# A hybrid decoder step: the delta-rule front moved beside the input projection, and the cache keys re-staged

## The reference, cut to what matters

```python
qa, ka, va, qb, kb, vb, fb, qc, kc, vc, zc, ac, bc, ud, vd = project(h, w_in)      # 1024 -> 3084 columns
o_a = combine_by_denominator([dilated(q, k, v, w, d) for (w, d) in ((128,1),(512,4),(2048,16))])  # A: sliding windows (SWA)
o_b = fox_attend(qb, kb_all, vb_all, cum_t, ...)                 # B: forgetting attention (FoX), all past keys
o_c, s_c, conv_c = gdn_branch(qc, kc, vc, ac, bc, ...)           # C: short conv, l2 norm, chunked delta rule
o_d, v_d = gmlp_branch(ud, vd, ws, bs, gv)                       # D: spatial gating
y = concat([norm(o_a), norm(o_b), norm(o_c) * silu(z_c), norm(o_d)]) @ w_out
```

```python
a_mat = where(strict, (k*beta) @ k.T * decay, 0);  t_mat = inverse(eye + a_mat)
u = t_mat @ (v * beta);  w = t_mat @ (k*beta*exp(gcum));  qk = (q @ k.T) * decay
v_new = u - w @ s;  o = (q*exp(g)) @ s + qk @ v_new;  s = s*exp(g_last) + (k*exp(g_last-g)).T @ v_new
```

## Time and profile before

| | |
|---|---|
| median of the runs (3) | 1573.7 us (1571.72 to 1576.14) |
| the profiled execution | 1572.86 us |
| its span, first to last instruction | 1571.0 us |
| mean granted TensorE clock | 0.884 |
| busy: PE, DVE, ACT, POOL | 1333.1, 921.0, 658.4, 217.5 us |
| chain that ended last | PE 75%, DVE 17%, issue 3%, ACT 3% |

### The profile page before, as it was taken

One profiled execution on the slowest core, in us unless ns is written; L12 is line 12 of the kernel. 1 busy time (PEld: TensorE's weight loads), 2 busy tenths in 40 slices (PEclk: granted clock), 3 DMA queues, 4 the chain that ended last, 5 costly groups with the idle time before them and its releaser, 6 DMA issues.

```text
span 1571.0 us, 27946 instructions
## 1 busy us (share of the span) xinstructions
PE 1333.1 (85%) x9968; PEld 1243.5 (79%) x9968; DVE 921.0 (59%) x1496; ACT 658.4 (42%) x1067; POOL 217.5 (14%) x176
## 2 busy tenths in 40 slices
PE   5999979977586579999979999798866757699998
PEld 5999979965474379999979999798754636699996
DVE  4666455485654655664466654555766554576633
ACT  4665443334200355654455644433340013565543
POOL 1000011023332220000010000200333331200000
PEclk9999989967687589999989999899577967799998
DMA  6565563354462234555645656453445513255553
GB/s 216 167 190 164 156 209 110 121 159 126 147 181 81 80 122 134 173 183 155 184 141 171 195 154 168 145 187 97 143 145 168 155 42 112 81 183 187 162 167 100
DMA packets 286118, 234.15 MB, mean 149 GB/s; under 512 B 19898, under 2 KB 282018, under 8 KB 286056
## 3 DMA queue, kind: packets, MB, share of 16 engines
q1 hardware_dynamic: 286056, 233.37, 48.7%
HBM read 228.65 MB, written 5.37 MB: 149 GB/s over the span
## 4 chain that ended last, share of the span: by engine, by line
PE 75%; DVE 17%; issue 3%; ACT 3%; DMA 1%; SPq 0%; DVEq 0%; POOLq 0%; ACTq 0%
PE ps L1397 19%; PE ps L1398 19%; PE ps L1399 19%; PE ps L1596 2%; PE ps L1694 2%; DVE s L1120 2%; DVE wlo L896 2%; DVE nlo L943 2%; PE ps L1541 1%; PE ps L1693 1%; DVE yt L926 1%; PE ps L1544 1%; ACT whi L591 1%; PE ps L1510 1%; PE ps L1684 1%
## 5 line engine op out<-in xcount | busy, mean ns | idle before, releaser
L1397 PE MATMUL ps<-nhi,whi 128*128 128x264 f32 x1936 | 564.2, 291 | 58.8 <-DVE nlo L943 38.9
L896 DVE TENSOR_TENSOR wlo<-raw,whi 128x1024 fp32r<-128x1024 f32 (+2 forms) x376 | 394.7, 1091 | 281.3 <-ACT whi L591 281.0
L1398 PE MATMUL ps<-nlo,whi 128*128 128x264 f32 x1936 | 558.1, 288 | 0.0
L1399 PE MATMUL ps<-nhi,wlo 128*128 128x264 f32 x1936 | 557.5, 288 | 0.0
L1397 PEld LDWEIGHTS ps<-nhi,whi 128*128 128x128 f32 x1936 | 375.0, 194 | 65.6 <-DVE nlo L943 32.1
L591 ACT ACTIVATE whi<-raw 128x1024 fp32r<-128x1024 f32 (+2 forms) x376 | 336.8, 945 | 180.5 <-PE ps L1399 107.7
L1398 PEld LDWEIGHTS ps<-nlo,whi 128*128 128x128 f32 x1936 | 375.3, 194 | 0.2
L1399 PEld LDWEIGHTS ps<-nhi,wlo 128*128 128x128 f32 x1936 | 372.7, 192 | 0.0
L1397 PE MATMUL ps<-hhi,whi 128*128 128x264 f32 x704 | 201.7, 286 | 9.1 <-DVE hlo L913 9.1
L1399 PE MATMUL ps<-hhi,wlo 128*128 128x264 f32 x704 | 200.8, 285 | 0.0
L1398 PE MATMUL ps<-hlo,whi 128*128 128x264 f32 x704 | 200.4, 285 | 0.0
(11 more groups left out here) (337 smaller groups left out, 1505.4 us busy)
## 6 DMA issues: line engine op xcount, KB each, us to landing
raw<-in_ffn_gate_dram SPq DMA_DIRECT2D x44, 1024.0 KB, 5.3
raw<-in_ffn_up_dram SPq DMA_DIRECT2D x44, 1024.0 KB, 5.4
raw<-in_ffn_down_dram SPq DMA_DIRECT2D x64, 704.0 KB, 4.5
raw<-in_w_in_dram SPq DMA_DIRECT2D x24, 1024.0 KB, 5.7
kslot<-in_cache_fox_k_dram SPq DMA_DIRECT2D x128, 128.0 KB, 2.7
vslot<-in_cache_fox_v_dram SPq DMA_DIRECT2D x128, 128.0 KB, 2.4
raw<-in_w_out_dram SPq DMA_DIRECT2D x8, 1024.0 KB, 5.1
kslot<-in_state_swa_k_dram SPq DMA_DIRECT2D x32, 128.0 KB, 2.6
```

The lines of the kernel that those rows point to most:

```text
L896: tt2(wlo[s][:, a:b], raw[s][:, a:b], whi[s][:, a:b].bitcast(F32), ALU.subtract).then_inc(S(f"w_lo{s}"), 1)
L1397: mm(out, wh, hi_, start=first, stop=False)
L1398: mm(out, wh, lo_, start=False, stop=False)
L1399: return mm(out, wl, hi_, start=False, stop=last)
```

## The change

1. `w_in` is loaded in another order of columns, in 6 pairs of full width (`WCOL`); q, k, v of the delta rule come first. The twelve gate columns (`fb`, `ac`, `bc`) have small weights of their own (`graw`, `ghi`, `glo`) that are loaded and split during FFN 1, and 24 matmuls of their own.
2. The weights lie at `w_at`; the delta rule's arrays (`at_`, `qkt`, `tt`, `tm`, `ys`, `kd`) now lie where `yt` and `sq8` are, so they can be used while `w_in` runs. After each `w_in` chunk TensorE calls `beside(j, s, i)`: gates, decays, gram matrices, inverse levels 0 to 2 and the token-major transposes. VectorE's and ScalarE's orders are interleaved with the weight tiles to match. The l2 norms of q and k go into the exponents of the decays (`lns`, `ex`); the first bias product in `scores(0)` (L1544) is left out.
3. FoX keys go in half-samples (4 pages, `keys(h)`, h = 0 to 15) through three slots `kh`; GpSimd multiplies in place and VectorE sums (`key_products`, `key_sums`). A slot is loaded again when its sum is done (`s_red >= h - 2`). Nine of the sixteen products stand ahead of `w_in` tiles in GpSimd's order.
4. GpSimd does `lo` for stream 1 of pairs 2 to 5, and two of the six convolutions.
5. SWA keys of all samples come in three transfers after `w_in` (`swk`), their products are made in place and `sample_swa` sums them. Maxima, shift, exp and the all-reduce are done once for all 8 samples.
6. Values are loaded for pairs of samples (16 page and 3 window transfers) into two slots, `vslot[0]` and `vslot[1]`, that lie over the weight buffers; `vslot[1]` lies over `swk`. `vals(1)` waits for all sums, `vals(p)` for `pv_mm >= p - 1`. `wo(0, 0)` is loaded after the last value product. Page numbers are read a second time for the values.
7. ScalarE loads the table set with both Ln and Exp after each group of Silu or Gelu; the multiplication of the second tile of the mixed output goes from GpSimd to VectorE.

The core of the diff, by engine:

```diff
# layout
+        swk = place("swk", [P, B, CACHE_T, GW], at=w_at)
+        vslot = [place(f"vslot{c}", [P, 2, NKT, GW + 1], at=w_at + 4 * B * CACHE_T * GW * (1 - c)) for c in range(2)]
+        at_ = place("at_", [P, 2, 512], at=k_at)
...
# SyncE
+    def keys(h):
+        b, slot = h // 2, h % 3
+        if h >= 3:
+            sp.wait_ge(S("s_red"), V("s_red", h - 2))
+        for k in range(4):
+            sp.dma_start(kh[:, slot, k, :], io["cache_fox_k"][bass.ds(page_of[b, 4 * (h % 2) + k], 1), l].rearrange("o p h d -> p (o h d)")).then_inc(S(f"k_in{slot}"), 16)
...
+    wi(2)
...
+    for h in range(3):
+        keys(h)
+    wi(3)
+    sp.wait_ge(S("gs_act"), V("gs_act", 3))
+    sp.dma_start(d_qf, smp[:, S_QB:S_QB + GW]).then_inc(S("q_pre"), 16)
...
+    for p in range(2):
+        queries(p)
...
+    read_pages(2)
+    wi(4)
+    for h in range(3, 6):
+        keys(h)
...
+    wi(5)
...
     sp.wait_ge(S("s_conv"), V("s_conv", 1))
...
+    for b in range(3, B):
+        read_pages(b)
+        if b == 4:
+            queries(2)
+        if b == 6:
+            queries(3)
+        for h in (2 * b, 2 * b + 1):
+            keys(h)
...
+    def window(dst, src, bs, sem):
+        a = io[src][bs, l].rearrange("b r h d -> b r (h d)")
+        sp.dma_start(dst(0, P), a[:, PAST - P:PAST, :].rearrange("b r d -> r b d")).then_inc(sem, 16)
...
+    def vals(p):
+        c = p % 2
+        if p == 1:
+            sp.wait_ge(S("s_red"), V("s_red", 24))
+        elif p:
+            sp.wait_ge(S("pv_mm"), V("pv_mm", p - 1))
...
+    for b in range(2):
+        read_pages(b)
...
+    sp.dma_start(q8[:, :, :], d_qs.unsqueeze(0).broadcast_to([P, B, GW])).then_inc(S("sk_in"), 16)
+    window(lambda k, n: swk[0:n, :, k, :], "state_swa_k", slice(0, B), S("sk_in"))
+    vals(0)
...
+    for p in range(1, 4):
+        for i in range(2):
+            read_pages(2 * p + i)
...
+        vals(p)
...
-    sp.wait_ge(S("s_red"), V("s_red", 16))
+    sp.wait_ge(S("pv_mm"), V("pv_mm", 4))
     wo(0, 0)
+    wo(0, 1)
...
# ScalarE, beside w_in
+    hi("wi", 2, 0)
+    for t in range(4):
+        act.wait_ge(S("conv_qk"), V("conv_qk", t + 1))
+        act.activation(conv_t[:, t, :], conv_t[:, t, :], ACT.Silu).then_inc(S("conv_silu"), 1)
+    load_table()
+    act.wait_ge(S("conv_silu"), V("conv_silu", 4))
+    act.activation(sqk[:, :, :], conv_t[:, 0:4, :], ACT.Square).then_inc(S("qk_sq"), 1)
+    hi("wi", 2, 1)
...
+    take_smp(3, 5)
+    hi("wi", 5, 0)
+    take_tok(3)
+    hi("wi", 5, 1)
...
+    act.wait_ge(S("s_red"), V("s_red", 16))
     softmax(0)
...
# GpSimd
+    def key_products(first, n):
+        for h in range(first, first + n):
+            b, slot = h // 2, h % 3
+            pool.wait_ge(S(f"k_in{slot}"), V(f"k_in{slot}", 64 * (h // 3 + 1)))
+            pool.wait_ge(S("q_in"), V("q_in", 16 * (b // 2 + 1)))
+            tt_(kh[:, slot, :, :], kh[:, slot, :, :], qf[:, b % 4, :].unsqueeze(1).broadcast_to([P, 4, GW]), ALU.mult).then_inc(S("kq"), 1)
+    lo("wi", 2, 1)
...
+    for j in range(3, WI_P):
+        key_products(3 * (j - 3), 3)
+        lo("wi", j, 1)
+    key_products(9, 7)
...
+    pool.wait_ge(S("sk_in"), V("sk_in", 64))
+    for b in range(B):
+        tt_(swk[:, b, :, :], swk[:, b, :, :], q8[:, b, :].unsqueeze(1).broadcast_to([P, CACHE_T, GW]), ALU.mult).then_inc(S("swq"), 1)
+    pool.wait_ge(S("s_red"), V("s_red", 24))
+    pool.wait_ge(S("slot_ones"), V("slot_ones", 1))
+    prepare(1)
+    pool.wait_ge(S("s_max"), V("s_max", 1))
+    pool.partition_all_reduce(pmax_all[:, :, :, :].rearrange("p a m h -> p (a m h)"),
+                              pmax[:, :, :, :].rearrange("p a m h -> p (a m h)"), P, RMAX).then_inc(S("s_max_all"), 1)
...
# VectorE
+    def key_sums(first, n):
+        for h in range(first, first + n):
+            dve.wait_ge(S("kq"), V("kq", h + 1))
+            g = 4 * (h % 2)
+            red(s13[:, h // 2, g:g + 4, :], kh[:, h % 3, :, :].rearrange("p g (h d) -> p g h d", h=H), AX.X, ALU.add).then_inc(S("s_red"), 1)
...
+    decays(0, at_, "strict_neg")
+    take(3, 0, 0)
+    decays(1, qkt, "causal")
+    take(3, 0, 1)
+    key_sums(0, 2)
+    lo("wi", 4, 0)
+    products(0)
+    take(3, 1, 0)
+    products(1)
...
+    take(3, 1, 1)
...
+    tt2(four(vb[:, :, :]), four(ps[:, 4:6, GW:2 * GW]), scale_(4), ALU.mult).then_inc(S("kv"), 1)
+    key_sums(2, 2)
+    for i in range(2):
+        take(4, 0, i)
+    lo("wi", 5, 0)
...
+    key_sums(4, 1)
...
+    masked_y(0)
+    for i in range(2):
+        take(4, 1, i)
+    update(0)
+    key_sums(5, 1)
...
+    update(4)
     masked(0, "fox_mask")
+    masked_y(5)
+    key_sums(11, 2)
+    update(5)
+    key_sums(13, 3)
...
+    sample_swa()
...
+    sample_shift()
+    attend_p(1)
...
# TensorE, after each w_in chunk
+    def beside(j, s, i):
+        if (j, s, i) == (1, 0, 0):
+            gates_turned()
+        elif (j, s, i) == (1, 1, 0):
+            cumulate()
+        elif (j, s, i) == (2, 0, 0):
+            more_rows()
+        elif (j, s, i) == (2, 0, 1):
+            head_norms()
+        elif (j, s, i) == (2, 1, 0):
+            rows_turned()
+        elif (j, s, i) == (2, 1, 1):
+            broadcast(0)
+        elif (j, s, i) == (3, 0, 0):
+            broadcast(1)
+        elif (j, s, i) == (3, 0, 1):
+            gram(0)
+        elif (j, s, i) == (3, 1, 0):
+            gram(1)
+        elif (j, s, i) == (3, 1, 1):
+            kv_turned()
+        elif (j, s, i) == (4, 0, 0):
+            inverse_turned()
+        elif (j, s, i) == (4, 0, 1):
+            pe.wait_ge(S("kv"), V("kv", 1))
+            token_major(2)
+        elif (j, s, i) == (4, 1, 0):
+            level_y(0)
+            pe.wait_ge(S("tok_act"), V("tok_act", TOK_AT[2] + 2))
+            sample_rows(2, 4)
+            sample_rows(3, 5)
+        elif (j, s, i) == (4, 1, 1):
+            pe.wait_ge(S("tok_act"), V("tok_act", SMP_AT[3] + 1))
+            level_z(0)
+        elif (j, s, i) == (5, 0, 0):
+            level_y(1)
+            token_major(3)
+        elif (j, s, i) == (5, 0, 1):
+            pe.wait_ge(S("tok_act"), V("tok_act", TOK_AT[3] + 2))
+            level_z(1)
+        elif (j, s, i) == (5, 1, 0):
+            level_y(2)
+            pe.wait_ge(S("pd_taken"), V("pd_taken", 12))
+            token_major(4)
+        elif (j, s, i) == (5, 1, 1):
+            pe.wait_ge(S("tok_act"), V("tok_act", TOK_AT[4] + 2))
+            level_z(2)
...
+    level_y(4)
...
+    scores(0, lambda a: proj[:, 6 + a, :], lambda a: proj[:, 8 + a, :])
+    level_z(4)
...
+    turn_p(1)
+    values(1, T_VA)
...
+    sample_values(0)
+    pe.wait_ge(S("p_state"), V("p_state", 4))
     for k in range(2):
         pe.wait_ge(S("sk"), V("sk", k + 1))
         mm(ps[:, 6, 0:HD], C("same_state"), sk_r[:, :], start=True, stop=True).then_inc(S("sk_mm"), 1)
+        sample_values(1 + k)
+    sample_values(3)
```

More of the change, by code:

```diff
@@ L117, in constants @@
     put("eps", np.full((P, 1), EPS))
+    put("eps64", np.full((P, 1), HD * EPS))
+    put("half", (i[:, None] // HD == np.arange(2)[None, :]))
     scale = np.ones((P, 1))
@@ L243, in build @@
+        conv_t = place("conv_t", [P, NCT, L])
+        vb = place("vb", [P, 2, GW])
+        here[0] = max(here[0], f_at + 8 * FT * N + 16 * N)
         f_end = here[0]
@@ new lines, in _ @@
+                    conv(1)
+                    dve.wait_ge(S("gate_act"), V("gate_act", 1))
+                    ch(stt(gate[:, :, :], gate_in[:, :, :], 0.0, gate_t[:, :, :], ALU.max, ALU.add))
+                    tt2(gate[:, :, :], gate[:, :, :], mul12[:, :].unsqueeze(1).broadcast_to([P, 3, 12]), ALU.mult).then_inc(S("gate_dve"), 1)
+                    for i in range(2):
+                        take(1, 0, i)
+                    conv(2)
+                    lo("wi", 2, 0)
+                    conv(3)
@@ new lines, in decays @@
+                    def decays(k, dst, mask):
+                        dve.wait_ge(S("bc_mm"), V("bc_mm", k + 1))
+                        for t in range(NT):
+                            for h in range(H):
+                                ins = stt(dst[:, t, h * P:(h + 1) * P], ps[:, 4 + 2 * k + h // 2, (h % 2) * L + t * P:(h % 2) * L + (t + 1) * P],
+                                          ex[:, t, 2, h:h + 1], C(mask), ALU.add, ALU.add)
+                        ins.then_inc(S("dt_masked"), 1)
@@ new lines, in _, with masked_y @@
+                    dve.wait_ge(S("mix_r"), V("mix_r", 1))
+                    ts(cv[:, 8, :], cv[:, 8, :], small[0:96, 0:1], C("q_scale", 96), ALU.mult, ALU.mult).then_inc(S("s_conv"), 1)
+                    key_sums(4, 1)
+                    def masked_y(k):
+                        for t in range(NT):
+                            dve.wait_ge(S(f"y_mm{t}"), V(f"y_mm{t}", k + 1))
+                            m = C(f"level{LEVELS[k]}").unsqueeze(1).broadcast_to([P, H, P])
+                            tt2(h4(ys[:, t, :]), h4(ps[:, 6 + t, :]), m, ALU.mult).then_inc(S(f"ys{t}"), 1)
@@ new lines, in _ @@
```

(20 more changed lines are left out.)

1162 lines of the change are left out of this document (558 added, 604 removed).

## The result

The changed kernel takes 1583.3 us (median of 7 runs, 1576.7 to 1588.2) against 1574.5 for the kernel before (7 runs); the ratio is 1.0054, with a 95% interval of 1.0035 to 1.0072. It is 0.5% slower, where 1542 us had been forecast. The profiled execution has a span of 1582.1 us, 11.1 more than before.

What follows compares the result with a forecast made beforehand. TensorE was taken to bound w_in, hand-overs between engines the mixers, SyncE's queue their later part. 11.3 us from w_out's earlier start plus 3.8 gave 15.1 a layer, 30 for two: 1572.9 to 1542 us, range 1500 to 1585.

Steps and rivals of the forecast that it cites:

- `w_in` with level 2: Input projection with inverse levels 0 to 2 beside it: ends at 376.5 us, from 312.5 plus added work and waits.
- What TensorE does beside the chunks: Transposes, three inverse levels, grams and broadcasts between w_in's chunks: 25 us of added TensorE work.
- The waits: TensorE waits made by the new orders beside w_in: 35.8 us, 39 with half of four slow starts.
- a slow start: After a long wait TensorE runs slowly at first: 1.0 to 1.6 us beyond the wait; 3.2 us counted.
- The rest of the mixers: From level 2's end to the last sum, set by SyncE's queue: 78.7 us, ending at 455.2.
- the last key issue: From level 2 to the last half-sample's issue, with levels 3, 4 and FoX scores: 38.4 us.
- 11.8 for the SWA keys: Loading SWA keys and broadcast queries, 3.5 MB at 5.7 us per 1 MB, two or three in flight: 11.8 us.
- The tail: From the last sum through values in two slots to w_out: 79.5 us.
- the walk's own 534.7: Start of w_out by the hand-walked orders if no cover fails; 532.5 was taken, against 543.8 before.
- Small edits: Three fewer table loads a layer at norms behind w_out: 3.8 us saved; the other small edits hidden or already counted.
- The rival of the lock: Beside w_in, GpSimd products stall VectorE through shared ports: 55 us a layer at worst; kernel at 1586 us; chance 0.2.
- Only moved: Work put beside w_in costs there what it saves later, values wait for SyncE's same queue: 1573 us; chance 0.1.

Runs made afterwards that it cites:

- the orders mended: The samples ahead kernel with the last pair of w_in tiles issued ahead of key half-samples 4 and 5 on SyncE: 1478.9 us, ratio 0.9395.
- round trip first: The changed kernel with the d_oc round trip issued on SyncE before the wait for the last value product, w_out weights and state stores: 1573.6 us, ratio 0.9994.
- samples ahead: The changed kernel with five joined edits and SWA keys before half-sample 12, plus the samples' part moved before the prompt's SWA part: 1506.4 us, ratio 0.9581.
- `lo` on GpSimd again: The samples ahead kernel with the four lo of stream 1 put back from VectorE to GpSimd: 1520.6 us, ratio 0.9652.
- the kernel with the sums back: The samples ahead kernel with sums 11 and 12 put back behind level 4's update on VectorE: 1513.5 us, ratio 0.9646.

## Why the prediction was wrong

The sum was to put `w_out` at 532.5; it is at 551.1, 18.6 us later in a layer. By its steps:

- **`w_in` with level 2.** Forecast 376.5, measured 376.0 (the update at 375.6 and 0.4 for itself). That it fits is luck, for two errors cancel. What TensorE does beside the chunks was 25 us in the sum; its busy time grew by 106.1 - 63.1 = 43 us, some 12 of it by the clock, which was 0.89 there and 1.00 before (an estimate, 11% of 106.1). The sum's own parts are more than 25 as well: 12.1, 4 and three levels at 2.05 twice, 12.3, are 28. The waits were 35.8; they are 19.3 in five and 19.9 in all. The places on GpSimd and the one at level 0's mask were right, the sizes about double. (The 1.6 us of a slow start is over what its rows give, 1.0 to 1.3; that is under 1 us in the sum.)
- **The rest of the mixers: the step that failed.** It said 78.7 us from level 2 to the last sum; it was 86.9 (376.0 to 462.9). By its terms: to the last key issue 42.5 for 38.4, small issues and page numbers 13.6 for 12.8, SWA keys 15.7 for 11.8, products and last sum 15.2 for 15.7. Two terms were too small by 4 us each. The first, 38.4, was costed as work with "a slot is free only after a sum": only 13.8 of it have rows, and what stands ahead of the sum in VectorE's order was not followed. The run that moved two sums shows what that order costs: the last key issue is then 25 us after level 2, not 42.5, the last sum of layer 0 is 14 us earlier, and 27 us are gone from the kernel. So the 38.4 came as near as 4 us without the mechanism behind it. Where the late sums no longer hold up the SWA keys, they cost 7 to 10, hardly clear of noise. The second, 11.8 for the SWA keys, took 5.7 us for 1 MB; here 1 MB took 10.4, with the values' transfers issued from 437.4 on beside them and the DMA engines full (share 1.0 from 437.4 to 447.7). No run separates the two.
- **The tail.** 79.5 in the sum, 88.2 measured. First value product 25.8 for 22, values in both slots 33.1 for 31.5, last product 6.7 for 5, from there to `w_out` 22.6 for 21.0. The largest misses are value products: the first took 8.6 us (480.1 to 488.7) and the last 6.7, where 5 stood for each, since TensorE ran them in part at its lower clock (granted 0.50 to 0.56 for the first). That is 5.3 of the 8.7 us. That SyncE's queue sets much of the rest was right: two of its orders (round trip and page numbers) gave their microseconds when they were moved. The round trip was missed: I took the last part "as before", though the change had put two issues and eight stores ahead of it; it costs 4.0 us.
- With the 2.2 us by which I had gone below the walk's own 534.7, 8.2 + 8.7 + 2.2 - 0.5 = 18.6.
- **Small edits.** The table loads behind `w_out`: 7.3 us late there, 4.1 at the first weights of the second FFN that follow the norm, so 3.2 for a forecast of 3.8.

So the walk had the right structure and its two last stretches about a tenth too short (8.2 of 78.7 and 8.7 of 79.5 us). The gain of 15 us a layer was the small difference of long chains that no row showed, 15 of 231 us (312.5 to 543.8); an error of that size in a chain of queues was to be expected, and the chance of 0.22 for slower was too low, as it counted little but the lock. The 1583.3 us lie just inside the 1500 to 1585 of the prediction, but its upper end stood there for the lock: that is luck too.

**The rivals.** The rival of the lock was nearest in time (1586), but not by its mechanism. In layer 0 of the profiled execution some 18 us of VectorE's time stand above nominal beside `w_in`, 12 of them in the two ropes, where the rival had 55; TensorE waits there for VectorE only for 3.2 us. The 8 of the larger rope are mostly not on the path by the run with the rope moved (the others I moved in no run). Taking the keys away from there made the kernel slower by 21 us, not faster, so the products there pay, although they delay `lo`. GpSimd's `lo` does cost (18 us alone, 11 to 14 in the faster kernel). By the four waits it is queued behind products that wait for their loads; the run also takes those `lo` out of VectorE's way, and what part that has was not measured. "Only moved" (1573) fits the mechanism best: what the front gave was taken up behind it. With the orders mended the kernel takes 1478.9 us, 96 less than the one before. How much of this the overlap beside `w_in` gives, no run shows: some of the edits could help the kernel before too, and one takes a part of the change back.

What stays open: the changed kernel's runs spread over 11.5 us, those of before over 5.2; in three of the profiled executions (round trip first, samples ahead, `lo` on GpSimd again) layer 0 lost 5 to 7 us more beside `w_in` than in the others. No run asks why, but their traces have the lock at that place. With the samples ahead, two `lo` of VectorE start at 286.4, just behind three products of GpSimd (285.8), and take 8.68 us; in the kernel with the sums back, whose orders are the same up to there, they start at 286.7, 4.6 us ahead of the products, and take 2.48. A second pair of `lo`, at 305.2, takes 6.59, and TensorE waits 8.0 us in all for what stands behind the two pairs. In the two others one step of 1.2 us takes 3.30 and one of 0.22 takes 1.9, which is 3.7 us of what they lost. So the lock can cost a layer several us when the two engines happen to meet.

## What to carry to other kernels

Where a buffer slot is freed by one engine and filled by a queue that serves others too, walk what stands ahead of the freeing instruction, not only its own cost: two sums of 1.2 us behind an update were worth 27 us while the SWA keys stood behind them in the queue, and 7 to 10 with the SWA keys ahead. When a stage is filled with other work, put loads that unblock the stage ahead of loads that only feed it (tiles before keys: 28 us), and give no step of the stage to an engine whose queue waits for transfers (18 us here). A forecast gain that is a few per cent of a long serial chain isn't a forecast of its sign.
